# Four modulation parts loaded into free activation space, and a rescaled difference of softmaxes, in a one-core kernel of two transformer blocks

## The reference, cut to what matters

```python
mod = jax.nn.silu(c) @ w_mod[l] + b_mod[l]          # 1024 -> 6 * 1024, for the latent and the context vector
sh1, sc1, gt1, sh2, sc2, gt2 = jnp.split(mod[:, None, :], N_MOD, axis=-1)
h = rms_norm_2(xl, g_pre_mix[l]) * (1.0 + sc1) + sh1
...
def diff_attend(q, k, v, lam):
    s = jnp.einsum('bhiqd,bhikd->bhiqk', q, k).astype(jnp.float32) * (HEAD_DIM ** -0.5)
    p = jax.nn.softmax(s, axis=-1)
    a = (p[:, :, 0] - lam * p[:, :, 1]).astype(v.dtype)
    return jnp.einsum('bhqk,bhkd->bhqd', a, v)
```

## Time and profile before

| what | value |
|---|---|
| median of three executions | 2739.88 us |
| the profiled execution | 2742.61 us |
| its span on the core | 2740.8 us |
| PE busy | 2564.3 us, 94% |
| DVE busy | 1635.2 us, 60% |
| ACT busy | 1274.2 us, 46% |
| mean granted PE clock | 0.974 |
| weight and other transfers | 393.64 MB, mean 144 GB/s |

### The profile page before, as it was taken

The page is one execution under the profiler, slowest core; times in us unless marked ns, Lnnn a source line. Parts: engine busy times, 40 slices in busy tenths (PEclk is TensorE's granted clock), DMA queues, the critical chain, the costliest instruction groups (busy, mean ns, idle before and its releaser), DMA issues.

```text
span 2740.8 us, 43247 instructions
## 1 busy us (share of the span) xinstructions
PE 2564.3 (94%) x16774; PEld 2154.4 (79%) x16774; DVE 1635.2 (60%) x2702; ACT 1274.2 (46%) x2372; POOL 209.5 (8%) x218
## 2 busy tenths in 40 slices
PE   7989889999988999999999999899999999987997
PEld 4744668888956899988875686588889999685997
DVE  2466465553687686668756763433326788764554
ACT  3355353433656665633336733422235644753443
POOL 3000100001201000324000001000001130000000
PEclk9999999999999999999999999999999999998999
DMA  7267222324554455534324433323245555445555
GB/s 277 86 228 270 72 66 95 99 88 127 164 190 157 149 182 172 175 101 146 115 92 143 140 100 135 125 93 99 88 112 162 170 172 175 154 135 200 176 173 142
DMA packets 119418, 393.64 MB, mean 144 GB/s; under 512 B 13728, under 2 KB 15776, under 8 KB 119136
## 3 DMA queue, kind: packets, MB, share of 16 engines
q1 hardware_dynamic: 117392, 386.47, 44.2%
q0 software_dynamic: 1872, 5.02, 0.7%
HBM read 390.39 MB, written 1.05 MB: 143 GB/s over the span
## 4 chain that ended last, share of the span: by engine, by line
PE 81%; DVE 9%; ACT 4%; DMA 4%; issue 1%; POOL 1%; SPq 0%; ACTq 0%; DVEq 0%; POOLq 0%
PE bank L570 23%; PE bank L571 23%; PE bank L572 23%; PE bank L719 2%; DMA ring<-in_w_mod 2%; PE bank L618 2%; DVE w_low L1617 2%; PE bank L729 2%; PE bank L649 1%; ACT w_high L984 1%; PE bank L744 1%; PE bank L742 1%; DVE smax L1858 1%; DVE conv_space L2118 1%; PE bank L679 1%
## 5 line engine op out<-in xcount | busy, mean ns | idle before, releaser
L570 PE MATMUL bank<-h_high,w_high 128*128 128x256 f32 (+1 forms) x3168 | 1058.4, 334 | 72.7 <-DVE w_low L1617 36.7
L1617 DVE TENSOR_TENSOR w_low<-ring,w_high 128x1024 fp32r<-128x1024 f32 (+2 forms) x604 | 684.1, 1134 | 610.5 <-ACT w_high L984 608.6
L572 PE MATMUL bank<-h_high,w_low 128*128 128x256 f32 (+1 forms) x3168 | 1041.1, 329 | 0.0
L571 PE MATMUL bank<-h_low,w_high 128*128 128x256 f32 (+1 forms) x3040 | 997.5, 328 | 0.0
L570 PEld LDWEIGHTS bank<-h_high,w_high 128*128 128x128 f32 x3168 | 610.8, 193 | 135.1 <-issue 58.3
L984 ACT CAST w_high<-ring 128x1024 fp32r<-128x1024 f32 (+2 forms) x604 | 574.1, 953 | 284.2 <-DMA ring<-in_w_down 161.6
L572 PEld LDWEIGHTS bank<-h_high,w_low 128*128 128x128 f32 x3168 | 610.7, 193 | 51.0
L571 PEld LDWEIGHTS bank<-h_low,w_high 128*128 128x128 f32 x3040 | 585.9, 193 | 48.9 <-issue 0.7
L570 PE MATMUL bank<-f_high,w_high 128*128 128x256 f32 (+1 forms) x880 | 269.2, 306 | 2.7 <-DVE w_low L1617 2.5
L571 PE MATMUL bank<-f_low,w_high 128*128 128x256 f32 (+1 forms) x880 | 267.7, 304 | 0.0
L572 PE MATMUL bank<-f_high,w_low 128*128 128x256 f32 (+1 forms) x880 | 267.6, 304 | 0.0
(11 more groups left out here) (230 smaller groups left out, 2625.2 us busy)
## 6 DMA issues: line engine op xcount, KB each, us to landing
ring<-in_w_mod SPq DMA_DIRECT2D x176, 512.0 KB, 4.4
ring<-in_w_up SPq DMA_DIRECT2D x176, 512.0 KB, 3.5
ring<-in_w_down SPq DMA_DIRECT2D x80, 384.0 KB, 3.1
ring<-in_w_down SPq DMA_DIRECT2D x80, 320.0 KB, 3.0
ring<-in_w_gate SPq DMA_DIRECT2D x48, 512.0 KB, 3.5
ring<-in_w_k SPq DMA_DIRECT2D x32, 512.0 KB, 3.5
ring<-in_w_v SPq DMA_DIRECT2D x32, 512.0 KB, 3.5
ring<-in_w_q SPq DMA_DIRECT2D x24, 512.0 KB, 3.5
```

The costliest lines, as they stand in the source:

```text
L570: pe.matmul(out, wh[:, cols], high, start=first, stop=False)
L571: pe.matmul(out, wh[:, cols], low, start=False, stop=False)
L572: ins = pe.matmul(out, wl[:, cols], high, start=False, stop=last)
L1617: v.tensor_tensor(wl[:, cols], raw[:, cols], wh[:, cols].bitcast(F32), ALU.subtract).then_inc(low_ready, 1)
```

## The change

Four parts (1_1_0, 2_1_0, 2_1_1, 2_1_2) leave the plan and so the ring. Their slabs go into eleven places of the space where the feed-forward hidden values lie later (`plan_spare`), loaded by SP behind certain slabs of mix1_0, merge and out, and the rest behind slab 3 of the following up product, each place again when the slab that was in it has been multiplied. PE multiplies them in the norms. The attentions keep the rest: global 1_0_1 alone, near 1_0_2 and 1_1_1, window and diff_0 as before, diff_1 none; outside the difference attentions the slabs are spread over all units. The first two slabs of up2, and of branch_1, are split earlier by the crossing of `later`, those of branch_0 by an explicit call before the last unit. `first_norm` on DVE makes the low half two chunks behind instead of one. In a difference unit, the first softmax is no longer scaled; the second gets the factor minus lambda times s0 over s1, and the output is scaled by 1/s0 where it is stored.

```diff
-BEGIN = 3
-            modulation(1, 1, 0, 1)
+            modulation(1, 1, 1)
...
-        modulation(2, l, *((1, 2) if l == 0 else (1,)))
+        if l == 0:
+            modulation(2, l, 1, 2)
...
-        if l == 1:
-            modulation(2, 1, 2)
-        if l == 0:
-            modulation(2, 1, 0)
...
+SPARE = 11
+def plan_spare():
+    order, loads = {}, {}
+    uses, last = [0] * SPARE, [0] * SPARE
+    for parts, places in ((("1_1_0",), [("mix1_0", g, 3) for g in (4, 5, 6)] + [("mix1_0", 7, 2), ("up1_0", 3, 5)]),
+                          (("2_1_0", "2_1_1"), [("merge_0", g, 1) for g in (5, 6, 7)] +
+                           [("out_0", g, 2) for g in (4, 5, 6, 7)] + [("up2_0", 3, 21)]),
+                          (("2_1_2",), [("merge_1", g, 1) for g in (5, 6, 7)] +
+                           [("out_1", g, 2) for g in (4, 5, 6, 7)] + [("up2_1", 3, 5)])):
...
+        spare = view("spare_slabs", R_1, SPARE * SLAB * P)
...
-        BESIDE = {"global": ("1_0_1", "1_0_2"), "near": ("1_1_0", "1_1_1"), "window": ("1_1_2", "2_0_0"),
-                  "diff_0": ("2_0_1", "2_0_2"), "diff_1": ("2_1_1",)}
+        BESIDE = {"global": ("1_0_1",), "near": ("1_0_2", "1_1_1"), "window": ("1_1_2", "2_0_0"),
+                  "diff_0": ("2_0_1", "2_0_2"), "diff_1": ()}
...
-            return min(slabs, u * slabs // (len(units) - 2))
+            return min(slabs, u * slabs // (len(units) - (2 if units[0]["diff"] else 0)))
...
# SP, behind a ring slab
+                        for one in SPARE_LOADS.get((L.name, at.g), ()) if isinstance(at.g, int) else ():
+                            _, slot, _, freed = SPARE_ORDER[one]
+                            if freed:
+                                sp.wait_ge(spare_done, freed)
+                            sp.dma_start(spare[:, slot * SLAB * P:(slot + 1) * SLAB * P],
+                                         T["w_mod" + one[0]][one[1] // 4, one[1] % 4]).then_inc(spare_landed[slot], 16)
...
# PE, the norm after mix1_0
-                    layer_norm(w)
+                    spare_slabs("1_1_0", range(3))
+                    row_stat(0, w, KC, 2)
+                    spare_slabs("1_1_0", range(3, 5))
+                    stat(lambda c: O[:, c, 0:w], KC, w, sq_ready, 3)
+                    spare_slabs("1_1_0", range(5, 16))
...
# PE, the norms after out_0 and out_1
+                def out_norm(c):
+                    if l == 0 and c < 6:
+                        spare_slabs("2_1_0" if c == 0 else "2_1_1", (15,) if c == 0 else (c - 1,))
+                    elif l == 1 and c < 4:
+                        spare_slabs("2_1_2", (12 + c,))
+                    elif l == 1 and c == 6:
+                        mod_turn("2_1_2")
...
-                mod_rows(part, range(2))
+                spare_slabs(part, range(2))
                 square_stat(f"out_{l}", QK[:, 8:16, :], 3)
-                mod_rows(part, range(2, 8))
-                stat(lambda c: QK[:, 8 + c, 0:w], KC, w, sq_ready, 3, lambda c: mod_slab(part, 8 + c))
+                spare_slabs(part, range(2, (15, 12)[l]))
+                stat(lambda c: QK[:, 8 + c, 0:w], KC, w, sq_ready, 3, out_norm)
+                if l == 0:
+                    spare_slabs("2_1_1", range(5, 16))
...
# ACT and DVE, modulate
-                    elif L is not None and rooted and step == BEGIN:
-                        begin(L, ahead)
...
# DVE, first_norm
-                for c in range(KC + 1):
+                for c in range(KC + 2):
...
-                    if c:
-                        low(lambda _: HL[:, c - 1, :], lambda _: O[:, c - 1, :], lambda _: HH[:, c - 1, :], 1, TOK)
+                    if c == 1:
+                        low_normed(0)
+                    elif c > 2:
+                        low_normed(c - 2)
...
# DVE, normalise and store of a difference unit
-                    own.inc(v.tensor_tensor(r1, r1, lam, ALU.mult))
-                    own.link(v.tensor_scalar(p0, p0, r0, None, ALU.mult))
+                    s0 = ssum[:, j % NS:j % NS + 1]
+                    own.link(v.scalar_tensor_tensor(r1, s0, lam, r1, ALU.mult, ALU.mult))
                     v.scalar_tensor_tensor(p1, p1, r1, p0, ALU.mult, ALU.add).then_inc(pr_ready, 1)
...
-                    v.tensor_copy(units[u]["out"], OUTB[:, 0:P]).then_inc(o_ready, 1)
+                    if units[u]["diff"]:
+                        r0 = srec[:, 2 * u % NS:2 * u % NS + 1]
+                        v.tensor_scalar(units[u]["out"], OUTB[:, 0:P], r0, None, ALU.mult).then_inc(o_ready, 1)
+                    else:
+                        v.tensor_copy(units[u]["out"], OUTB[:, 0:P]).then_inc(o_ready, 1)
```

More of the change, by code:

```diff
@@ L163, in plan_linears @@
     return {L.name: L for L in plan}, plan
+SPARE = 11
[7 more added lines that the diff above has]
+                           [("out_1", g, 2) for g in (4, 5, 6, 7)] + [("up2_1", 3, 5)])):
+        slabs = iter([(part, k) for part in parts for k in range(16)])
+        slot = 8
+        for name, g, count in places:
+            for _ in range(count):
+                one = next(slabs)
+                uses[slot] += 1
+                order[one] = (len(order) + 1, slot, uses[slot], last[slot])
+                last[slot] = len(order)
+                loads.setdefault((name, g), []).append(one)
+                slot = (slot + 1) % SPARE
+    return order, loads
 def build(nc, T):
     LIN, ORDER = plan_linears()
+    SPARE_ORDER, SPARE_LOADS = plan_spare()
     ctx = ExitStack()
@@ L270, in build @@
         slab_done = sem("slab_done")
+        spare_landed = [sem(f"spare_slab_landed{i}") for i in range(SPARE)]
+        spare_done = sem("spare_slab_done")
         emptied = {"scalar": sem("banks_emptied_by_scalar"), "vector": sem("banks_emptied_by_vector")}
@@ L761, in attend @@
                 if not diff:
-                    pe.wait_ge(rows_copied, n["rows"] + 2)
+                    pe.wait_ge(rows_copied, n["rows"] + len(beside))
                     for part in beside:
@@ L959, in _ @@
                     mod_turn("2_1_0")
+                    mod_turn("2_1_1")
                 else:
@@ L964, in _ @@
                 if l == 0:
+                    stored()
                     stored()
@@ L1255, in attend @@
                 banks, probt = (DIFF_SCORES, PROBT) if diff else (PAIR_SCORES, PAIR_PROBT)
-                half = next(u for u in range(len(units)) if mods_until(units, 16 * len(beside), u) >= 16)
+                halfway = [u for u in range(len(units)) if mods_until(units, 16 * len(beside), u) >= 16]
                 j0, u0, t0 = n["sub"], n["unit"], n["turned"]
@@ L1285, in attend @@
                 for u in range(len(units)):
-                    if u == half and len(beside) == 2:
+                    if len(beside) == 2 and u == halfway[0]:
                         mod_copy(beside[0])
@@ L1289, in attend @@
                         exps(u + AHEAD)
+                    if opens is not None and u == len(units) - 1:
+                        begin(LIN[opens], ahead)
                     copy(u)
@@ L1524, in high_branch @@
                         nc.scalar.copy(HH[:, c, 0:w], SC[:, c, 0:w]).then_inc(hh_ready, 1)
-                attend(f"diff_{l}", square_out)
+                attend(f"diff_{l}", square_out, opens="branch_0" if l == 0 else None)
                 act.wait_ge(silu_c, 1 + 4 * (l + 1))
                 high_branch(0)
-                begin(LIN[f"branch_{l}"], ahead)
                 act.wait_ge(emptied["scalar"], LIN[f"group_{l}"].empty0["scalar"] + 4)
@@ L1900, in attend @@
                         finish(c)
+                    if opens is not None and units[u]["diff"] and u == len(units) - 1:
+                        begin(LIN[opens], ahead)
                 store(len(units) - 1)
@@ L1903, in attend @@
                 n["unit"] += len(units)
-                if opens is not None:
+                if opens is not None and not units[0]["diff"]:
                     begin(LIN[opens], ahead)
@@ L2028, in _ @@
                 n["fh"] += FC
+                if l == 0:
+                    mod_store("1_1_0")
                 dve.wait_ge(x_ready, n["x"])
@@ L2157, in _ @@
                     products(f"gate_{l}_{i}", lambda at: conv_norm(8 * i + at.g))
-                attend(f"diff_{l}", minus_lam)
+                if l == 1:
+                    begin(LIN["branch_1"], ahead)
+                attend(f"diff_{l}", minus_lam, opens="branch_0" if l == 0 else None)
                 low(lambda c: CL[:, c, :], lambda c: SC[:, c, :], lambda c: HH[:, c, :], 4, w)
-                begin(LIN[f"branch_{l}"], ahead)
                 low(lambda c: CL[:, 4 + c, :], lambda c: SC[:, 4 + c, :], lambda c: HH[:, 4 + c, :], 4, w)
```

46 lines of the change are left out of this document (27 added, 19 removed).

## The result

Before and after, four executions each, taken side by side: 2739.7 us (2738.5 to 2742.7) and 2698.7 us (2696.2 to 2703.9). The ratio is 0.9851, 95% interval 0.9834 to 0.9868: 41.0 us less. The forecast was 2698. The profiled execution took 2698.55 us, its span is 2696.7, 44.1 less than before.

The account below looks back on a forecast made before the run. PE was taken as the bound, busy 2564.3 us, 94% of the span. The terms summed to 41.8 us, from the profiled 2742.6 to 2700.8, and with that execution 2.7 above the median, to 2698 us; range 2684 to 2720.

Parts of the forecast that it names:

- The two long stretches: From up1_0's first bank to the reciprocal ahead of diff_0: charges of 0.3 us for mod_turn/mod_store and 0.7 for window.
- Global and near: PE-bound attentions: 16 fewer slabs in global gain 10.0 us (5.0 to 11.7), spreading them in near 1.5 (0 to 3.1).
- The rival that latencies take over: Attentions don't follow a lighter PE: global 5.0, diff_1 1.5, diff_0 1.5; 11.8 us less gain, 2710 us; chance 0.12.
- Window: Window attention: slabs reach into the last two units, a loss of 0.7 us (0 to 2.0).
- The norm after mix1_0: Low half two chunks behind shortens chunk pairs to about 3.2 us, less slab delay: net gain 5.0 us (3.0 to 7.0).
- mod_store behind the up products: mod_turn and mod_store of 1_1_0 and 2_1_1 behind an up product: 0.3 us charged for both (0 to 2.0).
- diff_0: Fewer DVE passes in the chain 3.3 us, earlier split of branch_0's first slab 0.7: gain 4.0 (1.5 to 5.3).
- diff_1: Units of 2.65 us without slab gain 6.2, ends 2.0, new wait at group_1 costs 2.4: net 5.8 (1.5 to 9.0).
- The norm after out_0: Slabs ready early, last of 21 loads lands at 1729.6, PE done 1730.1: gain 7.0 us (0 to 8.0).
- out_1 and its norm: Extra loads cost out_1 2.0 us (0 to 7.0); norm opens up2_1 earlier, gain 9.5 net of that (4.5 to 11.5).
- the slower rate: Extra slabs come at 335 GB/s, 1.56 us each, instead of 409: 8.4 us less gain, 2706 us; chance 0.24.
- The clock: A denser PE is granted a lower mean clock; at 0.95 it costs 65 us, 2763 us; chance 0.04.

Follow-up runs that it names:

- e7: Changed kernel with 1_1_0 back in the attentions (global, near) and out of the norm after mix1_0: 2709.4 us, ratio 0.9868.
- e1: Changed kernel without ACT's crossing from group_1 to branch_1; branch_1's first two slabs cast before diff_1's last unit: 2694.9 us, ratio 0.9823.
- e2: Changed kernel with the eight slabs of 2_1_2 from behind slabs 4 to 7 of out_1 loaded behind slab 3: 2702.5 us, ratio 0.9859.
- e3: Changed kernel with the edits of e1 and e2 together: 2697.6 us, ratio 0.9845.
- e4: Changed kernel with only a quarter of each of ten 1_1_0 slabs multiplied in the gap before up1_0, loads kept: 2705.0 us, ratio 0.9866.
- f1: e1 with a twelfth place, five 2_1_2 loads beside out_1 instead of eight, seven in the norm behind, later turn and store: 2690.3 us, ratio 0.9814.
- f2: As f1, but two slabs of 2_1_2 loaded beside out_1 and ten in the norm behind it: 2691.6 us, ratio 0.9816.
- g1: f1 with only a quarter of each of ten 1_1_0 slabs multiplied in the gap before up1_0: 2698.6 us, ratio 0.9841.
- e5: Kernel before with one edit, DVE's low half two chunks behind in the norm after mix1_0: 2737.1 us against 2743.7, ratio 0.9976.
- e6: Kernel before with one edit, the difference of softmaxes scaled where it is stored: 2739.2 us, ratio 0.9983.
- e8: Changed kernel with 2_1_1 back in diff_1 and out of the norm after out_0, no crossing from group_1: 2699.4 us, ratio 0.9835.

## Why the prediction was right

The forecast was 41.9 us off the median, 41.0 came. In the profiled pair the nine rows of the table in which the change works gave 38.3 us where 42.8 were forecast. The two long stretches, for which 1.0 was charged, gave 4.3, which no run shows to be the change's, and the rest gave 1.5: that made 44.1, and the hit in the total owes luck to it. By its steps:

- **Global and near**: 10.5 and 1.2, forecast 10.0 and 1.5, with PE as the bound throughout. Right, and e7 shows the size. The rival that latencies take over is out: global has PE busy in 46.00 of 46.00. Of the 1.7 us that I took off the 11.7 for such waits 1.3 went to the clock instead: in e1, e2 and e3, where the same code has its high clock sooner (last section), global takes 51.2 to 51.4 us, 11.7 to 11.8 less than before.
- **Window**: no loss shows in it; the 2.7 us of its stretch are chance: the seven kernels e1 to e4, f1, f2 and g1, which don't differ from the changed one there, took 736.0 to 740.9 us for it, against 738.9 before.
- **The norm after mix1_0**: 6.2, forecast 5.0, with the mechanism as worked out (e5: 5.7 by the later low half alone). The half us charged for three slabs before the row sum was not there: from ACT's table load behind its last square to the reciprocal it is 3.81 us before, in the changed kernel and in e7. The 1.6 us of the stretch behind are not the edit's as far as is shown (e5, e6).
- **mod_store behind the up products**: nothing shows of the 0.3.
- **diff_0**: 3.2, forecast 4.0. DVE left the chain but for the start and one pass at 1484.38 (rescaling 2.9, forecast 3.3); the early split was mis-sized, 0.3 instead of 0.7.
- **diff_1**: units of 2.57 us, forecast 2.65, against 3.09. The 2.0 for the ends was too much: from scores to branch_1 6.6 came, not 8.2. The wait at group_1 came as worked out, 2.3 for 2.4; what it costs further in diff_1 by the clock, 0.9, I had not (e1).
- **The norm after out_0**: 5.0, forecast 7.0. The rate was nearly right: the last slabs come every 1.28 us, all eighteen behind slab 14 every (1708.78 - 1684.87) / 18 = 1.33, against the rival's 1.56. The start of the queue was wrong. PE had slab 14, for which I took 2.7 us from request to landing as in the earlier trace rows, at 1684.87, 1685.67 - 1684.87 = 0.8 us before the first square; I had 3.05 before it. With others in flight the spare slabs took longer to land, as the view of their tile says (median 7.6 us):

```profile
DMA to landing us min/median/max: 4.2/7.6/14.3
```

- **out_1 and its norm**: 4.4 lost, forecast 2.0, and 12.3 gained, forecast 11.5. I let the loads collide with the first slabs of up2_1 at the end; they collided with those of out_1 from slab 4 on. Sixteen slabs are asked for in twenty us, in which fifteen can land at 1.28 each, and f1 and f2 with fewer give it back; it is 3.2 to 4.4 by the spread of out_1. How much of the norm's gain comes from the slabs' new place and how much from the earlier split of up2 was not run apart.
- **Rivals**: the slower rate is out by the rows every 1.28 us and by 403 GB/s. The clock did not fall with a denser PE: the mean is 0.983 against 0.974. Where it fell, in diff_1, a wait stood ahead of it (e1). The Trainium skill gives about 358 GB/s as one core's limit ("DMA: Bandwidth & Descriptors", Specifications); this trace disagrees a second time, by the same 403.

## What to carry to other kernels

Work moved into a gap is free for PE only as long as its transfers fit the gap too: count the slabs that must land there and in the stage ahead, and multiply by the slab's time at full rate before you count what the old place gains. Of the four parts moved here 1_1_0 paid in full (e7), 2_1_0, which stayed in its norm and only got its loads earlier, goes with a norm 28.7 - 20.8 = 7.9 us shorter (e8, the earlier split of up2 in it), 2_1_2 paid less what out_1 lost, and 2_1_1 paid nothing until the crossing was taken away (e1, f1). Preload spread between the ring's own requests, not in a bunch ahead of them; and when an item goes out of an ordered plan, look at what its neighbours now do across the place where it stood. And before a clock reading is put down to an edit, look for the same reading in kernels without the edit: here e6 undid what e5 seemed to show.

## What the runs showed of the hardware

- A transfer's time from request to landing is no constant of the chip: 2.5 to 3.2 us for branch_1's slabs before, a median of 7.6 and up to 14.3 for the preloaded ones, at some 1.28 us between landings. 14.3 / 1.28 gives an estimated eleven transfers under way.
- A wait of 2.97 us ahead of diff_1 cost 0.9 us more behind it through the granted clock, and such a fall stands in all five executions with the crossing, in none of the five without it, where the wait is 0.66 us (e1). A low clock behind the opening of up1_0 (0.83) came in one of two kernels with the same pauses of 0.8 to 1.3 us, so the pauses alone don't set it. Filling the gap ahead of that opening with 11 slabs gave at most 0.5 (19.1 and 18.9 without, 18.6 with).
- The same code from the root ahead of global to the reciprocal behind mix1_0 took 181.9 to 185.2 us in ten executions of kernels that don't differ there, 185.2 in three of them and 182 in four. What differs is the granted clock. The ten us from global's first scores on, in the changed kernel (185.2) and then in e1 (181.9):

```profile
152.84:162.84 10.00, 9.41 (x45) 4.43 (x46) 6.13 (x16) 5.64 (x17) 0.00 (x0) 0.60 0.19 54
```

```profile
152.13:162.13 10.00, 9.23 (x64) 4.62 (x64) 6.50 (x17) 6.46 (x20) 0.00 (x0) 0.80 0.24 68
```

  The low level lasts until 8 us after the first scores in the three of 185.2 and until 3 to 4 us in e1, e3, f1 and the kernel before. In near it comes back for 3 to 4 us in those three, behind a wait of 2.36 us that e1 has too, without the fall. What decides between the two no run shows.
- So a single profile can't price a term below some 3 us in such a stretch. Diff_0 and diff_1 repeated within 0.1 (diff_1 with the crossing within 0.4), the norm after out_1 within 0.6, the norm after out_0 and out_1 within 1.4.
